# A chunked recurrent scan over four streams: pairs half a tile apart in place of single streams a quarter apart

## What is computed

```python
def step(S, inp):
    r_t, w_t, kk_t, b_t, k_t, v_t = inp
    sa = jnp.einsum('bhvk,bhk->bhv', S, -kk_t)
    S = S * w_t[:, :, None, :] + sa[..., None] * b_t[:, :, None, :] + v_t[..., None] * k_t[:, :, None, :]
    y = jnp.einsum('bhvk,bhk->bhv', S, r_t) if emit else None
    return S, y
S, ys = lax.scan(step, S0, xs, reverse=reverse)
```

## The kernel before

| phase | PE | DVE | ACT / POOL |
|---|---|---|---|
| k0 | lora products, L2387 | | ACT: four tanh L2516, L2519 |
| k1 | | running sum, L2606 | POOL: L2561 |
| k2 | | L2610 | ACT: three exps L2524 to L2526; POOL: L2565 |
| k3 | | scaling, L2616 to L2621 | |
| k4 | pair products, L2399 | | POOL: L2569 to L2571 |
| k5 | | masking the pairs, L2625 | |
| k6 | transposes L2410, L2415 | L2632, L2634, L2636 | ACT: L2530, L2533 |
| k7, k9, k11, k13, k15 | inverse, product x, L2427 | mask, L2642 | |
| k8, k10, k12, k14, k16 | inverse, product m, L2441 / L2443 | add, L2654, and transpose, L2658 (k16: L2649) | |
| k17 to k19, k20 to k22 | per chunk: L2456; L2462; L2471/L2472 | L2663 in the first, state L2670 in the third | POOL: L2581; ACT: L2540 in the second |
| k23 | start of the outputs, L2482 | | |
| k24 | outputs, L2495, L2497, L2500 | L2681, L2683 or L2685 | |

## Time and profile before

### The profile page before, as it was taken

The page is one execution under the profiler, slowest core; times in us unless marked ns, Lnnn a source line. Parts: engine busy times, 40 slices in busy tenths (PEclk is TensorE's granted clock), DMA queues, the critical chain, the costliest instruction groups (busy, mean ns, idle before and its releaser), DMA issues. The chain is left out here.

```text
span 4684.1 us, 80619 instructions
## 1 busy us (share of the span) xinstructions
PE 4090.9 (87%) x33798; PEld 3351.7 (72%) x33798; DVE 2731.3 (58%) x4351; ACT 1734.2 (37%) x2825; POOL 331.2 (7%) x419
## 2 busy tenths in 40 slices
PE   6999986997898998699479877889999587999997
PEld 5878864886786667388367766768888466888886
DVE  2347736885675553688546102647787644556556
ACT  2136622774363442377537211223233112222222
POOL 0000000220000000022000000013333001000000
PEclk9999997998999999799789998978999698999998
DMA  2100027995000002799500112000000121111111
GB/s 101 45 10 2 2 107 274 376 392 193 19 2 1 1 1 78 290 371 397 206 20 2 55 63 72 28 13 3 3 4 3 61 109 63 36 54 37 54 46 41
DMA packets 139157, 425.54 MB, mean 91 GB/s; under 512 B 14661, under 2 KB 50381, under 8 KB 114221
## 3 DMA queue, kind: packets, MB, share of 16 engines
q1 hardware_dynamic: 129580, 386.83, 21.4%
q0 software_dynamic: 9216, 33.56, 2.8%
HBM read 370.03 MB, written 50.33 MB: 90 GB/s over the span
## 5 line engine op out<-in xcount | busy, mean ns | idle before, releaser
L557 PE MATMUL psum<-weight_parts,h_parts 128*128 128x512 f32 (+2 forms) x2880 | 601.5, 371 | 45.8 <-DVE weight_parts L703 29.4
L557 PEld LDWEIGHTS psum<-weight_parts,h_parts 128*128 128x128 f32 x2880 | 508.3, 192 | 133.1 <-DVE weight_parts L703 30.5
L1520 DVE TENSOR_TENSOR weight_parts<-weights_raw,weight_parts 128x2048 fp32r<-128x2048 f32 x192 | 431.6, 2288 | 57.2 <-ACT weight_parts L1490 56.4
L911 ACT ACTIVATE scores<-scores,softmax_stats 128x1024 f32<-128x1024 f32 (+2 forms) x288 | 307.9, 1069 | 331.5 <-DVE softmax_stats L956 331.4
L1490 ACT ACTIVATE weight_parts<-weights_raw 128x2048 fp32r<-128x2048 f32 x192 | 360.4, 1919 | 71.3 <-DMA weights_raw<-in_moe_w_up 42.2
L1428 PE MATMUL psum<-weight_parts,picked_parts 128*128 128x512 f32 x1536 | 364.6, 397 | 15.6 <-DVE weight_parts L1520 10.8
L1901 PE MATMUL psum<-h_parts,up_parts 128*128 128x512 f32 x1536 | 355.4, 393 | 11.0 <-DVE up_parts L1976 11.0
L1917 PE MATMUL psum<-down_parts,hidden_parts 128*128 128x512 f32 x1536 | 353.5, 391 | 6.7 <-DVE down_parts L1981 6.7
L703 DVE TENSOR_TENSOR weight_parts<-weights_raw,weight_parts 128x2048 fp32r<-128x2048 f32 (+2 forms) x48 | 100.7, 2098 | 428.2 <-ACT weight_parts L612 428.1
L1428 PEld LDWEIGHTS psum<-weight_parts,picked_parts 128*128 128x128 f32 x1536 | 291.1, 191 | 79.3 <-issue 11.5
L1901 PEld LDWEIGHTS psum<-h_parts,up_parts 128*128 128x128 f32 x1536 | 291.3, 190 | 72.8 <-DVE up_parts L1976 11.8
(11 more groups left out here) (439 smaller groups left out, 7109.1 us busy)
## 6 DMA issues: line engine op xcount, KB each, us to landing
weights_raw<-in_moe_w_gate SPq DMA_DIRECT2D x64, 1024.0 KB, 13.5
weights_raw<-in_moe_w_up SPq DMA_DIRECT2D x64, 1024.0 KB, 13.9
weights_raw<-in_moe_w_down SPq DMA_DIRECT2D x64, 1024.0 KB, 12.7
w_ada<-in_w_ada SPq DMA_DIRECT2D x12, 2048.0 KB, 10.6
up_raw<-in_w_mlp_up SPq DMA_DIRECT2D x16, 1024.0 KB, 7.3
down_raw<-in_w_mlp_down SPq DMA_DIRECT2D x16, 1024.0 KB, 5.0
weights_raw<-in_even_w_in SPq DMA_DIRECT2D x10, 1024.0 KB, 5.1
weights_raw<-in_w_in SPq DMA_DIRECT2D x10, 1024.0 KB, 5.0
```

Source lines behind the costliest of these rows:

```text
L557: last = pe.matmul(ps[:, t, 0:width(n)], cols[:, i, KP * h + k, t * P:(t + 1) * P], part[:, n % 2, j, k, 0:width(n)], start=(h == 0 and m ...
L911: act.activation(s_b[:, i % 2, a, 0:w], s_b[:, i % 2, a, 0:w], ACT.Exp, bias=st[:, i % 4, 0, a:a + 1], scale=-1.0, accum_out=st[:, i % 4, ...
L1520: dve.tensor_tensor(part[:, n % PART_SLOTS, 1], raw[:, n % RAW_SLOTS], part[:, n % PART_SLOTS, 0].bitcast(F32), ALU.subtract).then_inc(low, 1)
```

## The change

`take_turns` takes pairs of programs and starts both of a pair at once; the lag is `PHASES // 2 = 12`. The pairs are (s0, s2) and (s1, s3): both directions of one group of heads. On SP nothing changes; the four lists of PE, ACT, POOL and DVE are all reordered by it, and no instruction is added or removed.

```diff
 def take_turns(programs, lag):
     live = []
-    for program in programs:
-        live.append(program)
+    for first, second in programs:
+        live += [first, second]
         for _ in range(lag):
             for p in list(live):
                 if next(p, "end") == "end":
...
-        LAG = PHASES // 4
+        LAG = PHASES // 2
...
-            take_turns([stream(*x) for x in every], LAG)
+            take_turns([(stream(*every[g]), stream(*every[2 + g])) for g in (0, 1)], LAG)
```

## The result

The change makes the kernel slower: 4804.8 us median against 4670.8 in the same set of runs, a ratio of 1.028 with a 95% interval of 1.0265 to 1.0295. The direction was forecast and the order of the waits too; the +69 us were half of the 134 that came, and 4804.8 lies just inside the upper end of the range, 4810. One of the change's four executions took 5619 us at a mean clock of 0.70 and is a slow one that is left out of the ratio.

The account below looks back on a forecast made before the run. PE was taken to bound the scan's middle, 93% busy, with DVE 13 points behind. Ends -11, idle time +67 and clock +13 summed to +69 us, taking the median from 4673.45 to 4742; range 4662 to 4810.

Parts of the forecast that it names:

- What bounds the kernel now: Scan's middle: PE sets the time, 93% busy, DVE at 80%; gathering DVE work in one place makes DVE the bound there.
- the hand schedule: Half a tile of the middle laid out at full clock: 30.1 us in place of 26.4; chance 0.62.
- Two of its signs: Scan: PE's waits for L2621 above 1.3 us per half; prediction wrong if PE stays above 90% busy with four streams.
- The ends, -11 us: Start and end of the scan: -17 us until all four streams run, +6 us after the last k1.
- The middle, +67 from idle time and +13 from the clock: Nine tiles, 18 halves: +3.7 us of PE idle each; clock falls cost 31 us where before had about 18.
- The idle time of 5.6 us per half: PE's waits in half a tile of the middle, beside 24.5 us of PE work; before had 1.9 us idle.
- POOL isn't in the chain.: POOL's k1 and k4 steps double, but end before the DVE work that stands ahead of their users.
- One fall of the clock per half, at 1.7 us: Before k4 PE has little work, so its clock falls once in each of 18 halves: 31 us.
- The factor of 1.38: PE work takes 1.38 times as long at low clock, from 180 against 249 products in 10 us.
- The low-clock rival: The clock stays low for half of each half tile, 84 us in place of 31: 4795; chance 0.14.
- The rivals on the other side: PE stays fed, 4662 or 4653, or the pair costs and gives little, 4660 to 4687; same 0.12, faster 0.12.

Follow-up runs that it names:

- the unread products: The change plus two 128x128 matmuls on PE, whose result nobody reads, in each stream's k2, k3 and k4: 4742.9 us, ratio 1.0157.
- starts of 0, 4, 8, 12: The kernel before with its four streams, in the change's order, starting in rounds 0, 4, 8, 12 instead of 0, 6, 12, 18: 4782.0 us, ratio 1.0238.
- starts of 0, 3, 12, 15: The change's pairs with 3 rounds between the two of a pair, in place of starts 0, 0, 12, 12: 4752.3 us, ratio 1.0165.

## Why the prediction was right, and where its size was off

**What bounds the kernel now, and that the new bound is DVE's burst: right in the order of the waits, not in their sum.** The waits of the hand schedule came one by one, behind the instructions that it named. Two of its signs went the other way. PE's waits for L2621 were to be above 1.3 us per half; they sum to 22.2 us in the scan, 1.1 per half, less than the 25.9 before. And the forecast called itself wrong if PE stayed above 90% busy with four streams: it is busy 540.25 of 599.43 us, 90.1%, since the same products keep it busy longer at the low clock.

**The ends, -11 us: -3.** The first part shrank by 15 us as the text had it by 17; the last part is 51 us, not 47, with a mean clock of 0.63 where it was 0.80 before.

**The middle, +67 from idle time and +13 from the clock: +116.** PE's idle time there rose by 27 us and its busy time by 89. So the idle term was 40 us too large and the clock's 76 us too small, and it is partly luck that the sum came as near as it did. Three steps failed here.

- *The idle time of 5.6 us per half.* It was laid out at full clock. The waits of the half shown sum to 3.5 us, with PE's work between them stretched by the low clock. Against 1.9 before that is 1.6 us more per half, 29 us over 18 halves, which fits the 27.
- *"POOL isn't in the chain."* It ends in time, but it works while DVE does the second k3, and the two share something: 0.42 becomes 0.83 us. That made the second k3 2.77 us and not 1.53. Taking the overlap away gives back 85 us. Without it the forecast of 4742 would have erred on the high side (4720), but its idle time even so: that kernel's middle has 55 us of it where 32.6 + 67 were forecast.
- *One fall of the clock per half, at 1.7 us.* There is one per half, but the price was read from falls that ended within one period. In the change the clock stays low for 16.6 us, all through the stretch in which DVE leads, and comes back only with the dense levels; two halves never come back and cost 10 us more each. The half takes 33 us where 31.8 were forecast, and 599 us are 36 more than 563.

The factor of 1.38 for work at the low clock was also read too low. It compares products in 10 us of time, but at full clock PE was busy only 8.87 of these. For each busy microsecond it is 28.1 products against 18.0, a factor of 1.56. The two stretches don't hold the same products, so this is rough too. The rival's price of 4795 rests on the same 1.38.

The Trainium skill's rule, in "TensorE: Matmul & The Clock Gate", section "HAM oscillation", that bursts with waits between keep falling back to the low clock, resembles the change's half tiles: they begin each DVE-led stretch at 0.50, and the unread products that fill the waits restore 62 us. The page's case has waits of 3 to 5 us for DMAs, though, and the longest wait in the half shown here is 1.42 us. That waits are the cause is not enough for starts of 0, 4, 8, 12, whose waits are nearly those of before and whose clock is 0.76.

The low-clock rival, priced at 4795, was the nearest single case; it had the right length of the low stretch. The rivals on the other side fell: PE's queue passes nothing, and DVE's total over a half, although small enough, doesn't help while the order asks for it at once.

Open: which property of PE's work lets the clock fall where PE doesn't wait; why one pairing has two halves wholly at the low level and the other none; and what the change would cost at full clock without added work.

## What to carry to other kernels

When streams are staggered over phases of unequal load, spread the starts over the whole cycle; a spacing that saves rounds at the ends but bunches heavy phases lost more in the middle here: in the change a quarter of it by waits and three quarters by TensorE's clock, with starts of 0, 4, 8, 12 nearly all by the clock. Before you double an engine's step, look at which other engine runs at that moment, not only at whether it ends in time. And where PE waits a known half microsecond behind another engine, two unread products there can be worth more than they cost; here they gave 0.24%, and three gave nothing.

## What the runs showed of the hardware

- DVE steps with two SBUF operands of 128x256 fp32 took 0.83 us in place of 0.42 while POOL ran its own two-operand step, and POOL's took 0.80 in place of 0.61; keeping them apart restored both and took 85 us off the kernel. The Trainium skill, "GPSIMD Engine Reference", section "Specifications", says that POOL shares its SBUF interfaces with DVE and contends with steps of two SBUF inputs; the trace agrees.
- The granted clock stood at 0.50 in windows in which PE was busy without a gap (the one at 3360 above), mostly with fp32 products on 64x64 quarters of the array. With starts of 0, 3, 12, 15 it fell to 0.50 after 13 us of PE busy without a gap. Unread 128x128 products lifted the scan's clock from 0.69 to 0.90 and 0.98.
